# Two transformer blocks on one core: a half-length Fourier table, a rotation from doubled product columns, and context weights in order of use

## The reference, cut to what matters

```python
def fourier_mix(z):                       # z: 256 tokens x 4 groups x 128
    y = jnp.fft.fft2(zg, axes=(1, 3), norm='ortho').real
...
def axial_rope(x, cos, sin):              # 32 channels of each head, and of the shared key
    x1, x2 = xf[..., :half], xf[..., half:]
    return jnp.concatenate([x1 * cos - x2 * sin, x2 * cos + x1 * sin], axis=-1)
...
y_f = fourier_mix(f)
mla_k, mla_v = mla_keys_values(ckv, kr, g_kv, w_uk, w_uv, rope)
mla_q = mla_queries(cq, g_q, w_uq, w_qr, rope)
```

## Time and profile before

| | |
|---|---|
| median of 3 runs | 2861.45 us (2854.47 to 2870.16) |
| the profiled execution, its time | 2861.8 us |
| its span, first to last instruction | 2859.9 us |
| TensorE busy | 2656.0 us, 93% of the span |
| TensorE's mean granted clock | 0.973 of 2.4 GHz |
| transfers | 764.83 MB, mean 267 GB/s |

### The profile page before, as it was taken

The page is one execution under the profiler, slowest core; times in us unless marked ns, Lnnn a source line. Parts: engine busy times, 40 slices in busy tenths (PEclk is TensorE's granted clock), DMA queues, the critical chain, the costliest instruction groups (busy, mean ns, idle before and its releaser), DMA issues.

```text
span 2859.9 us, 34002 instructions
## 1 busy us (share of the span) xinstructions
PE 2656.0 (93%) x13722; PEld 1836.0 (64%) x13722; DVE 802.0 (28%) x1937; ACT 455.9 (16%) x971; POOL 74.8 (3%) x144
## 2 busy tenths in 40 slices
PE   6997999889999998999998999999999999999998
PEld 2555455456667764546555667687788545787887
DVE  1345113231112252111111335416542225313002
ACT  2132102121111012000000214301000123201001
POOL 0000000000000000000000000000000000000000
PEclk9998999999999999999999999999999999999999
DMA  9795998899998739999999832233675311333430
GB/s 395 320 375 201 377 401 360 346 384 417 407 404 345 304 117 383 422 418 420 422 416 422 340 145 80 89 148 145 267 287 213 118 59 59 118 145 120 157 138 16
DMA packets 117626, 764.83 MB, mean 267 GB/s; under 512 B 12832, under 2 KB 15648, under 8 KB 34272
## 3 DMA queue, kind: packets, MB, share of 16 engines
q1 hardware_dynamic: 94400, 680.57, 59.0%
q0 software_dynamic: 20224, 74.26, 6.7%
q10 hardware_dynamic: 2848, 7.83, 0.7%
HBM read 759.20 MB, written 3.41 MB: 267 GB/s over the span
## 4 chain that ended last, share of the span: by engine, by line
PE 79%; DMA 12%; DVE 5%; issue 2%; ACT 1%; SPq 1%; ACTq 0%; DVEq 0%
PE bank L587 77%; DMA ring<-in_stream 11%; PE bank L903 1%; PE bank L892 1%; PE bank L591 1%; SPq L466 1%; DVE MX L2039 1%; DVE work L1950 1%; DMA work<-in_stream 1%; DVE work L2056 0%; ACT work L1520 0%; ACT A L1530 0%; ACT work L1452 0%; DVE A L1958 0%; DVE NM L2044 0%
## 5 line engine op out<-in xcount | busy, mean ns | idle before, releaser
L587 PE MATMUL bank<-A,ring 128*128 128x256 f32 (+1 forms) x3088 | 711.4, 390 | 17.1 <-issue 9.6
L587 PEld LDWEIGHTS bank<-A,ring 128*128 128x128 f32 x3088 | 588.2, 191 | 137.5 <-issue 50.3
L587 PE MATMUL bank<-ring,A 128*32 128x512 f32 (+3 forms) x2304 | 397.4, 623 | 64.3 <-DMA ring<-in_stream 55.5
L587 PE MATMUL bank<-work,ring 128*128 128x256 f32 x1696 | 385.3, 383 | 5.7 <-DVE work L2549 2.1
L587 PEld LDWEIGHTS bank<-work,ring 128*128 128x128 f32 x1696 | 322.5, 191 | 56.9 <-issue 3.9
L587 PE MATMUL bank<-work 128*64 128x128 f32 (+5 forms) x2084 | 320.3, 332 | 27.7 <-DMA work<-in_stream 7.6
L587 PEld LDWEIGHTS bank<-ring,A 128*32 128x32 f32 (+2 forms) x2304 | 124.6, 127 | 318.8 <-issue 216.7
L587 PEld LDWEIGHTS bank<-work 128*128 128x128 f32 (+2 forms) x2084 | 243.7, 173 | 81.7 <-issue 42.5
L587 PE MATMUL bank<-A,work 128*128 128x256 f32 x1280 | 289.3, 383 | 4.0 <-issue 3.3
L587 PEld LDWEIGHTS bank<-A,work 128*128 128x128 f32 x1280 | 241.1, 191 | 59.3 <-issue 25.6
L587 PE MATMUL bank<-work,A 128*128 128x256 f32 (+2 forms) x416 | 130.5, 458 | 11.3 <-DVE X L2256 4.3
(11 more groups left out here) (288 smaller groups left out, 1543.4 us busy)
## 6 DMA issues: line engine op xcount, KB each, us to landing
ring<-in_stream SPq DMA_DIRECT2D x648, 1024.0 KB, 12.7
work<-in_stream POOLq DMA_DIRECT2D x134, 512.0 KB, 8.8
X<-in_xt ACTq DMA_DIRECT2D x1, 2048.0 KB, 13.8
spill<-work ACTq DMA_DIRECT2D x3, 512.0 KB, 9.8
work<-spill POOLq DMA_DIRECT2D x3, 512.0 KB, 4.8
tab_sb<-in_tab_a ACTq DMA_DIRECT2D x1, 1120.0 KB, 18.5
X<-in_ctx2t ACTq DMA_DIRECT2D x1, 1024.0 KB, 15.1
out<-X SPq DMA_DIRECT2D x4, 256.0 KB, 2.3
```

The costliest lines, as they stand in the source:

```text
L587: return pay(pe.matmul(o, w, x, start=start, stop=stop, tile_position=place), tells)
```

## The change

Four edits, the first two in both layers of the second block:

1. The Fourier table holds 129 cosine and 127 sine columns, 256 in all. `dft` (tokens and context) has 256 columns instead of 512; its copy by ScalarE has 256. `idft` is two products side by side in the bank (`two_parts`: 129 columns by `cd`, 127 by `sd`) instead of two of 256 columns added up. VectorE builds all 256 columns from it (`both_halves`: a copy of 129 columns, waited for; a subtraction written in reversed order; an addition) instead of one copy of 256.
2. The weights of mq and of the key have the exchanged halves in rows 96 to 127, which held zeros, so that the product yields them. `krope` and `qrope` are gone. VectorE reads rows 96 to 127 and writes rows 64 to 95.
3. The context's quarters of `l0_up` come in the order tiles 24 to 31, 0 to 7, 16 to 23, 8 to 15; the first is freed after mv1, the second after mq3, the rest after mq7.
4. The steps: a2 2 to 1, a4 3 to 4, c5 2 to 1, d5 2 to 3. So nv0 moves to b2 and t0 to c2, every later step up to t9 moves one place, t9 comes to a4, and gb0 moves from c5 to d5.

The tables shrink: the context's from 1280 to 768 columns, the tokens' from 1920 to 1280.

```diff
@@ -105,8 +105,8 @@
-    "a2": 2, "b2": 2, "c2": 4, "d2": 5, "a4": 3, "b4": 4, "c4": 7, "d4": 4, "a5": 6, "b5": 5, "c5": 2,
-    "d5": 2, "a6": 2, "b6": 2, "c6": 2, "d6": 2, "a7": 2, "b7": 2, "c7": 2, "d7": 2, "a8": 2, "b8": 2,
+    "a2": 1, "b2": 2, "c2": 4, "d2": 5, "a4": 4, "b4": 4, "c4": 7, "d4": 4, "a5": 6, "b5": 5, "c5": 1,
+    "d5": 3, "a6": 2, "b6": 2, "c6": 2, "d6": 2, "a7": 2, "b7": 2, "c7": 2, "d7": 2, "a8": 2, "b8": 2,
@@ -118,7 +118,10 @@
-EARLY, QLAG = 2, 2
+HALF = T // 2
+EARLY = 2
@@ -135,10 +138,7 @@
-        out += one(f"low{l}", "DDDD") + early + one(f"krope{l}", "D")
-        for j in range(8 + QLAG):
-            out += [(f"mq{l}", j, "A")] if j < 8 else []
-            out += [(f"qrope{l}", j - QLAG, "D")] if j >= QLAG else []
+        out += one(f"low{l}", "DDDD") + early + one(f"mq{l}", "A" * 8)
@@ -231,7 +231,8 @@
-    QUARTERS += [(places(_stage, "E")[t // TILES], t % TILES // QTILES) for t in range(0, _tiles, QTILES)]
+    _q = [(places(_stage, "E")[t // TILES], t % TILES // QTILES) for t in range(0, _tiles, QTILES)]
+    QUARTERS += [_q[i] for i in (3, 0, 2, 1)] if _stage == "l0_up" else _q
@@ -252,7 +253,7 @@
-TC, N_TC = columns([("dft", TB * 2 * T), ("cd", P), ("sd", P), ("cos", T), ("sin", T), ("swap", P)])
+TC, N_TC = columns([("dft", TB * T), ("cd", P), ("sd", P), ("cos", T), ("sin", T)])
@@ -339,7 +340,7 @@
-        FT, FU = wk(0, 4, 512), wk(2048, 8, 512)
+        FT, FU = wk(0, 4, 512), wk(2048, 4, T)
@@ -368,7 +369,7 @@
-        cFT, cFU, cTAB = wk(S0, TB, 512), wk(S0 + 1024, 4, 512), wk(S0 + 3072, 1280)
+        cFT, cFU, cTAB = wk(S0, TB, 512), wk(S0 + 1024, 4, T), wk(S0 + 3072, 768)
@@ -537,7 +538,7 @@
-            pool.dma_start(cTAB, tab_b[:, 0:1280]).then_inc(c_tab_in, 16)
+            pool.dma_start(cTAB, tab_b[:, 0:768]).then_inc(c_tab_in, 16)
@@ -606,6 +607,11 @@
+            def two_parts(b, wave, u):
+                mm(b[:, 0:HALF + 1], wave(0), u[:, 0:HALF + 1], True, True)
+                return mm(b[:, HALF + 1:T], wave(1), u[:, HALF + 1:T], True, True, tells=True)
@@ -673,12 +679,11 @@
-                    clinear(("dft", g), 512, lambda k: cFT[:, k, g * P:(g + 1) * P], lambda k: cTAB[:, k * 512:(k + 1) * 512], TB)
+                    clinear(("dft", g), T, lambda k: cFT[:, k, g * P:(g + 1) * P], lambda k: cTAB[:, k * T:(k + 1) * T], TB)
-                    clinear(("idft", g), T, lambda k: cTAB[:, 1024 + k * P:1024 + (k + 1) * P],
-                            lambda k: cFU[:, g, k * T:(k + 1) * T], 2)
+                    two_parts(cgroup("idft", g), lambda k: cTAB[:, 512 + k * P:512 + (k + 1) * P], cFU[:, g, :]).then_inc(c_lin, 1)
@@ -739,6 +744,8 @@
+                    if blk:
+                        free("l0_up", 8)
@@ -746,7 +753,7 @@
-                            free("l0_up", 8 if h == 3 else 32)
+                            free("l0_up", 16 if h == 3 else 32)
@@ -1250,14 +1257,13 @@
-                    linear(f"dft{l}", g, 2 * T, lambda k: FT[:, k, g * P:(g + 1) * P],
-                           lambda k: tab(TC, "dft", k * 2 * T, 2 * T), TB)
+                    linear(f"dft{l}", g, T, lambda k: FT[:, k, g * P:(g + 1) * P],
+                           lambda k: tab(TC, "dft", k * T, T), TB)
-                    linear(f"idft{l}", j, T, lambda k: tab(TC, "cd" if k == 0 else "sd"),
-                           lambda k: FU[:, j, k * T:(k + 1) * T], 2)
+                    two_parts(group(f"idft{l}", j), lambda k: tab(TC, "sd" if k else "cd"), FU[:, j, :]).then_inc(lin_ready, 1)
@@ -1300,16 +1306,10 @@
-                wait_taken(pe, f"low{l}", 3)
-                linear(f"krope{l}", 0, T, lambda k: tab(TC, "swap"), lambda k: LOW[:, 3, 0:T], 1)
-                for j in range(8 + QLAG):
-                    if j < 8:
-                        linear(f"mq{l}", j, w, lambda k: tile(st, 2 * j + k), lambda k: LOW[:, k, 0:w], 2)
-                    if j >= QLAG:
-                        wait_taken(pe, f"mq{l}", j - QLAG)
-                        linear(f"qrope{l}", j - QLAG, T, lambda k: tab(TC, "swap"), lambda k: A[:, j - QLAG, 0:T], 1)
+                for j in range(8):
+                    linear(f"mq{l}", j, w, lambda k: tile(st, 2 * j + k), lambda k: LOW[:, k, 0:w], 2)
@@ -1422,7 +1422,7 @@
-                    act.activation(cFU[:, g, :], ctake("dft", g), ACT.Copy).then_inc(c_taken["A"], 1)
+                    act.activation(cFU[:, g, :], ctake("dft", g)[:, 0:T], ACT.Copy).then_inc(c_taken["A"], 1)
@@ -1714,7 +1714,7 @@
-                    act.activation(FU[:, j, :], take(f"dft{l}", j, 512), ACT.Copy).then_inc(taken["A"], 1)
+                    act.activation(FU[:, j, :], take(f"dft{l}", j, T), ACT.Copy).then_inc(taken["A"], 1)
@@ -1772,6 +1772,13 @@
+            def both_halves(y, b):
+                odd = b[:, HALF + 1:T]
+                link(dve.tensor_copy(y[:, 0:HALF + 1], b[:, 0:HALF + 1]))
+                dve.tensor_tensor(y[:, T - 1:HALF:-1], y[:, 1:HALF], odd, ALU.subtract)
+                return dve.tensor_tensor(y[:, 1:HALF], y[:, 1:HALF], odd, ALU.add)
@@ -1831,7 +1838,7 @@
-                    dve.tensor_copy(cY0[:, g, :], ctake("idft", g)[:, 0:T]).then_inc(c_taken["D"], 1)
+                    both_halves(cY0[:, g, :], ctake("idft", g)).then_inc(c_taken["D"], 1)
@@ -2500,7 +2507,7 @@
-                    dve.tensor_copy(YB[0][:, j, 0:T], take(f"idft{l}", j, T)).then_inc(taken["D"], 1)
+                    both_halves(YB[0][:, j, 0:T], take(f"idft{l}", j)).then_inc(taken["D"], 1)
@@ -2517,17 +2524,17 @@
-                rot = slice(64, 96)
-                cos, sin = tab(TC, "cos")[rot, :], tab(TC, "sin")[rot, :]
-                dve.tensor_tensor(QT[rot, 0, :], take(f"krope{l}", 0, T)[rot, :], sin, ALU.mult).then_inc(taken["D"], 1)
+                rot, far = slice(64, 96), slice(96, 128)
+                cos, sin = tab(TC, "cos")[rot, :], tab(TC, "sin")[far, :]
+                dve.wait_ge(tabb_in, 16)
+                dve.tensor_tensor(QT[rot, 0, :], LOW[far, 3, 0:T], sin, ALU.mult)
-                dve.wait_ge(taken["D"], TAKEN[GROUP[f"krope{l}", 0]])
-                    dve.tensor_tensor(QT[rot, j % 2, :], take(f"qrope{l}", j, T)[rot, :], sin, ALU.mult).then_inc(taken["D"], 1)
+                    dve.tensor_tensor(QT[rot, j % 2, :], A[far, j, 0:T], sin, ALU.mult)
@@ -2649,11 +2656,12 @@
-        krp[:, 64:96] = kr
+        krp[:, 64:96], krp[:, 96:112], krp[:, 112:128] = kr, kr[:, 16:], kr[:, :16]
-        q[:, :, 64:96] = I["w_qr_2"][l].reshape(256, HEADS, 32)
+        q[:, :, 64:96] = qr = I["w_qr_2"][l].reshape(256, HEADS, 32)
+        q[:, :, 96:112], q[:, :, 112:128] = qr[:, :, 16:], qr[:, :, :16]
@@ -2729,16 +2737,12 @@
-    sin[64:80], sin[80:96] = -np.sin(ang), np.sin(ang)
+    sin[96:112], sin[112:128] = -np.sin(ang), np.sin(ang)
-    sw = np.zeros((P, P), np.float32)
-    i = np.arange(16)
-    sw[80 + i, 64 + i] = sw[64 + i, 80 + i] = 1
-    q(tc, TC, "swap", sw)
-    q(tc, TC, "dft", np.concatenate([np.cos(a), np.sin(a)], 1).reshape(TB, P, 2 * T).transpose(1, 0, 2))
+    q(tc, TC, "dft", np.concatenate([np.cos(a)[:, :HALF + 1], np.sin(a)[:, 1:HALF]], 1).reshape(TB, P, T).transpose(1, 0, 2))

```

## The result

| | before | changed |
|---|---|---|
| median (runs) | 2862.41 us (6) | 2843.66 us (6, 2842.75 to 2848.05) |
| ratio of the times, 95% interval | | 0.9938 (0.9925 to 0.9951) |
| profiled execution, its span | 2859.9 us | 2844.0 us |

By the ratio the changed kernel is 17.7 us faster (14 to 21). The forecast was 24, which gave 2838; the time lies in the stated range (2827 to 2853), but just outside what the likeliest case alone gave (2832 to 2843).

A forecast was written before the change was run, and what follows sets the result against it. It took TensorE, busy 93% of the span, as the bound, with gains passing only as far as idle transfer time allowed. Tokens 9.7, context 0 + 9 + 5.4 made 24.1 us off 2861.8: about 2838, range 2827 to 2853.

The forecast's parts named there:

- likeliest case: Whole kernel: the forecast itself, 24.1 us less, about 2838, giving 2832 to 2843 us; chance 45%.
- Fourier, tokens, layer 1: Token Fourier branch, layer 1: nq 3.5 us earlier, less 1.0 charged for a lower clock; gain 2.5 us.
- Fourier, tokens, layer 0: Token Fourier branch, layer 0: nq 1.4 us earlier, but TensorE idles over 4 us and pays 1.9; loss 0.5 us.
- rotation, layer 0: Layer 0 attention: VectorE bounds at 1.12 us a head; attention starts at 1782.2 instead of 1786.41, gain 4.2 us.
- rotation, layer 1: Layer 1 attention: eight qrope products go, TensorE stays the bound; gain 3.5 us.
- context, units 1, 2 and start of 4: First expert stage: up product 4 earlier, nv0 7 later, a step 2.7 less; zero, between -3 and +3 us.
- mv0 in unit 4: Unit 4: the 7.6 us quarter wait and 2.0 for the half clock go; 9 us, all passing through.
- gb0 in unit 5: Unit 5: gb0 behind the down product frees strips some 10 us earlier; idle transfer time passes 5.4 us.
- rest of the stage: After unit 5 each unit waits for the ring, and the shift of 9 + 5.4 us stays.
- less from the context: Rival: the a2 order costs 3 us and unit 5's shift does not pass; 15.7 us gained, 2846; chance 21%.
- transfers swallow all the context gain: Rival, expert stage: context gain becomes ring waits of units 4 to 8; 9.7 us remain, 2852; chance 15%.
- Signs that I had named: Expected in the profile: quarter wait, unit 2's 10 us ring wait, 36 fewer records, transfer rates, nq and attention starts.

The follow-up runs named there:

- second profile: The changed kernel run once more, nothing altered; 2842.45 us, ratio 0.9938 to the kernel before.
- no_quarters: The changed kernel with the l0_up quarters and their frees in the order of before; 2849.35 us, ratio 0.9953 to the kernel before.
- mv0_in_c4: The changed kernel with b4 4 to 3 and c4 7 to 8, so mv0 comes behind unit 4's turn and gather; 2838.84 us, ratio 0.9917 to before.
- tokens_reordered: The changed kernel with layer 0's Fourier columns built before the context's mean is subtracted, and two rotation heads per VectorE instruction; 2841.09 us, ratio 0.9920 to before.
- nv0: The kernel before with only a2 2 to 1 and a4 3 to 4 (nv0 behind unit 2's up product); 2862.81 us, ratio 1.0002.
- context_edits: The kernel before with all edits to the order of quarters and steps, none to Fourier or rotation; 2854.07 us, ratio 0.9971.

## Why the prediction was nearly right, step by step

| step | forecast, us | measured, us |
|---|---|---|
| Fourier, tokens, layer 1 | 2.5 | 3.9 |
| Fourier, tokens, layer 0 | -0.5 | 1.9 - 2.6 - 1.65 = -2.4 |
| rotation, layer 0 | 4.2 | 2.7 |
| rotation, layer 1 | 3.5 | 3.5 |
| context, units 1, 2 and start of 4 | 0 (-3 to 3) | 2.3 / 0.2 |
| mv0 in unit 4 | 9 | 2.4 / 2.7 |
| gb0 in unit 5 | 5.4 | 5.1 / 5.5 |
| rest of the stage | 0 | 0.9 / 0.8 |
| sum | 24.1 | 18.4 / 16.9 |

Measured numbers are the distance of like instructions in the changed kernel's profile from those of before, as it changes over the step (context: first / second profile; tokens: first). gb0 is read to the gate product of unit 6. That the 1.65 in the second line belongs to the change is not shown (last section). The times say 17.7. The spans differ by 15.9 only, because the run of the changed kernel lost 6.3 us ahead of unit 0 and that of before some 4 between 960 and 1100, both where nothing was changed.

**The step that failed** is "the wait is gone, 9 us (of the 9.6 I leave 0.6 to the short waits of the norm there)". The quarter was late, but the norm was late next, and I priced it from nothing: its two reciprocals of 1.75 and 1.69 us and three scalings in 1.28 stood in VectorE's timeline under the wait for the quarter, and TensorE must have their result before mv0. Taken from the trace, the step would have been 545.0 less 542.7, 2.3 us, with the clock still at 0.50, and the forecast 17.4 us or 2844. no_quarters and mv0_in_c4 bracket it: putting the old order back costs 2.5 at mv0, hiding the norm as well gives 5.3 to 5.8 at the place. The outcome is that of the rival "less from the context", but not by its causes: gb0's 5.4 came, and the context up to unit 4 gave 2.3 or 0.2 where that rival had -3. So the range held because this miss, the largest, is smaller than what the range left room for; the other misses nearly cancel.

**Transfers.** gb0's number came out, but it doesn't show that idle transfer time set it. Against the rows just ahead of gb0 the down product of unit 5 came 10.4 us earlier, and 5.1 to 5.5 were left at the gate product of unit 6 (654.97 before, 651.43 after), ahead of any further wait for the ring. That is close to the 5.4 us of idle transfers in the earlier trace rows, and as close to what TensorE saved by itself: the wait of 3.27 is gone, and gb0 runs in 3.72 us instead of 5.38. The forecast said that TensorE's work was only moved, and left this out. The last half strip of unit 6's up product was waited for until 682.88 before and 677.20 after, which against the same rows is 7.3 us earlier: the transfers gave more than the 5.4. What is shown is that they didn't take the gain back. The rival that transfers swallow all the context gain is out.

**Unit 2.** The order of things was as forecast, the new ring wait 6.6 instead of 10 and nv0 on the path. It came out between 0 and 2 us, inside the stated 3. The zero is made of two things: 2.5 to 3.1 us from the shorter Fourier, and 1.3 to 2.3 lost by nv0's move. The rest up to mv0 is the last ring wait of unit 4's up product, 0.4 to 2.3 us in profiles of the changed kernel's code there, which is more than half of the difference between 2.3 and 0.2.

**Fourier.** `both_halves` is cheaper than priced, 0.72 a group and not 0.83; writing in reversed order costs the same 0.29 as the addition's 0.28. By the formula of the Trainium skill ("VectorE: DVE Perf Modes", "The TRN2 errata") the three operations were to take 0.87, an estimate; their lengths add up to 0.85, so page and rows agree on each, but they overlap. Layer 1 gave more because its 1.72 us of idle didn't touch the clock, for which I had charged 1.0. Layer 0 gave less: the direction was right (a loss, since VectorE is late and TensorE idles 3.94 us), but the slow stretch cost 2.6 and a second one 1.65, where I had 1.9 in all. tokens_reordered takes away the wait and the slow stretch by changing the order on VectorE alone.

**Rotation, layer 0.** VectorE is the bound, as said, but I took 1.12 us a head from two heads of the kernel before; now a head costs 1.32 to 1.34. Each operation lasts as long as it did (0.41 to 0.42), but the distance between them grew. Eight heads are 1.7 us more, and that is the miss.

**Signs that I had named.** 36 records fewer: yes. Quarter wait under 1 us: yes, none. nq of layer 1 after 7.5 us: 7.20. Attention of layer 0 after 14.6: 16.14. Transfer rate at 636 to 646 near 420: yes; at 561 to 571: no, 156; mv0 had come only 2.4 us earlier.

## What to carry to other kernels

When a wait is removed, look under it: list everything that the released instruction needs, and take the second-latest arrival from the trace. Here it was 2.3 us behind the first, and the rest of the gain lay in a table entry that puts a turn over it. Where a faster engine then idles for some us, count what it loses to the clock afterwards as well, and see whether the late engine has work in its queue that could come second. Before laying two profiles over each other, find an instruction ahead of every edit and start from it.

## What was not expected of the hardware

- **The clock differs from run to run in the same code.** Ahead of every edit two profiles of one kernel lie 4.3 us apart at unit 0. After ring waits of 2.5 and 2.7 us the clock stayed in one run and fell in another; after 3.94 us before nq it fell in six of six profiles, after 1.72 in none of twelve (layer 1 in nine, layer 0 in three). The Trainium skill ("TensorE: Matmul & The Clock Gate", "HAM oscillation") describes the half rate coming back after each wait for data; the six rows with 3.94 agree, and those with 2.5 and 2.7 show that much the same wait need not bring it.
- **A second slow stretch, cause open.** In the six profiles with a slow nq the clock fell again some 50 us later, behind idle times of 1.35 and 0.73 us in unchanged code. It looks like an effect of the slow nq, but nv0 and context_edits, whose nq ran at the full clock, fell at the same place (0.66 at 1720 to 1725 and at 1705 to 1710), and the other six profiles with a full-clock nq did not. This is the changed kernel:

```profile
1705.00:1710.00 5.00, 3.41 (x13) 1.51 (x14) 3.27 (x10) 3.29 (x9) 0.00 (x0) 0.79 0.64 264
```

- **On VectorE, some operations start before the one ahead has ended.** In `both_halves` the third starts 0.20 after the second, which lasts 0.29. In the rotation before, L2531 started 0.34 after L2530, which lasts 0.41, and so did the next L2530 behind L2532; in the changed kernel those distances are 0.44 and 0.45, longer than the 0.42 of one operation. A read from a bank is not what decides: the four L2162 of the earlier trace rows read and write SBUF only, last 0.285 each and take 0.90 together. What is new in the rotation is that its first operation reads partitions 96 to 127 between operations that read 64 to 95. No run separates that from the bank that it no longer reads, so the cause stays open. In length the move from 96 to 127 to 64 to 95 costs nothing, 0.42 us.
- **Twice the columns cost 1.6 times.** 32x256 takes 0.42 us, 32x512 0.69.
